# Second mixing: latent products and norms run among the delta rule's state steps, attention heads among the first branch's tiles; equal shapes together

## The reference, cut to what matters

```python
proj = h @ w_in[l]
q_lat, kv_lat, k_pe, gq, gk, gv, ga, gb, gz, gates = jnp.split(proj, split_at, axis=-1)
y_mla = mla_branch(q_lat, kv_lat, k_pe, ...) @ w_o_mla[l]
y_gdn = gated_deltanet_branch(concat([gq, gk, gv]), ga, gb, gz, ...) @ w_o_gdn[l]
mixed = (gate_mla * y_mla + gate_gdn * y_gdn) @ w_out[l]
# mla_branch, 8 heads:
q = (rmsnorm(q_lat, g_q) @ w_uq)        # 768 -> 8 x (128 + 64), the 64 rotated by position
kv = (rmsnorm(kv_lat, g_kv) @ w_ukv)    # 256 -> 8 x (128 keys + 128 values)
s = (qn @ k_nope.T + qp @ k_pe.T) * scale; p = softmax(mask(s)); o = p @ v
# gated_deltanet_branch, 8 chunks of 64 tokens, 8 heads, one step per chunk:
v_new = u_n - w_n @ state
o = qd @ state + a_n @ v_new
state = state * cd + kd.T @ v_new
# then o = rmsnorm(o, g_out) * silu(z)
```

## Time and profile before

| | before |
|---|---|
| median of 3 executions | 3745.99 us (3742.91 to 3747.77) |
| profiled execution, its own time | 3751.27 us |
| span of the profile | 3749.5 us |
| TensorE busy, share of the span | 3443.9 us, 92% |
| VectorE busy | 2047.9 us, 55% |
| ScalarE busy | 1329.6 us, 35% |
| mean granted TensorE clock | 0.924 |
| share of the chain that ended last: TensorE, VectorE, ScalarE, DMA | 79%, 11%, 4%, 3% |

### The profile page before, as it was taken

How to read it: one execution, slowest core, us unless ns; L and a number is a source line. 1 busy time by engine, 2 the same in 40 slices (tenths; PEclk the granted TensorE clock), 3 DMA queues, 4 the chain that set the end, 5 groups by cost and what they waited for, 6 DMA issues and landing times.

```text
span 3749.5 us, 41096 instructions
## 1 busy us (share of the span) xinstructions
PE 3443.9 (92%) x16313; PEld 2794.3 (75%) x16313; DVE 2047.9 (55%) x3550; ACT 1329.6 (35%) x2342; POOL 522.2 (14%) x541
## 2 busy tenths in 40 slices
PE   5897997998999999999899987989988798889998
PEld 3466577998888888888788866877775563578887
DVE  2455598785887887888555335554432323343332
ACT  1222123886444444444322234545340212223221
POOL 0000100995222222221000000000000000000000
PEclk9886899999999999999799988999995697799999
DMA  5330523456998989997255321222211121022222
GB/s 176 136 107 12 174 95 108 176 199 248 349 324 324 330 322 332 319 330 269 95 186 185 126 94 59 71 70 85 71 49 37 55 68 68 31 82 91 100 91 79
DMA packets 189679, 574.02 MB, mean 153 GB/s; under 512 B 16368, under 2 KB 80496, under 8 KB 171056
## 3 DMA queue, kind: packets, MB, share of 16 engines
q1 hardware_dynamic: 152160, 369.80, 28.4%
q0 software_dynamic: 37328, 201.61, 14.6%
HBM read 523.69 MB, written 47.64 MB: 152 GB/s over the span
## 4 chain that ended last, share of the span: by engine, by line
PE 79%; DVE 11%; ACT 4%; DMA 3%; POOL 1%; issue 1%; SPq 0%; DVEq 0%; ACTq 0%; POOLq 0%
PE ps L228 10%; PE ps L229 10%; PE ps L230 10%; PE ps L237 5%; PE ps L1439 5%; PE ps L1440 5%; PE ps L1438 5%; PE ps L1200 3%; PE ps L1202 3%; PE ps L1201 3%; PE ps L312 2%; PE ps L168 1%; DVE Wl L220 1%; DMA hidden_dram<-peerg_HS 1%; PE ps L509 1%; PE ps L2150 1%
## 5 line engine op out<-in xcount | busy, mean ns | idle before, releaser
L220 DVE TENSOR_TENSOR Wl<-W,Wh 128x1024 fp32r<-128x1024 f32 x363 | 438.2, 1208 | 740.1 <-ACT Wh L214 740.1
L214 ACT ACTIVATE Wh<-W 128x1024 fp32r<-128x1024 f32 x363 | 377.6, 1041 | 595.9 <-PE ps L230 575.1
L1200 PE MATMUL ps<-peer_Hh,Wh 128*128 128x384 f32 x1024 | 348.6, 340 | 14.1 <-DVE Wl L220 14.1
L1202 PE MATMUL ps<-peer_Hh,Wl 128*128 128x384 f32 x1024 | 345.0, 337 | 0.0
L1201 PE MATMUL ps<-peer_Hl,Wh 128*128 128x384 f32 x1024 | 344.6, 337 | 0.0
L1438 PE MATMUL ps<-peerv_VH,peer_HTh 128*128 128x512 f32 x768 | 299.8, 390 | 9.6 <-DVE peer_HTl L1501 9.6
L1440 PE MATMUL ps<-peerv_VH,peer_HTl 128*128 128x512 f32 x768 | 301.1, 392 | 0.0
L1439 PE MATMUL ps<-peerv_VL,peer_HTh 128*128 128x512 f32 x768 | 301.1, 392 | 0.0
L1408 POOL DMA_INDIRECT peerv_UV<-peer_uv,peer_EX x128 | 209.4, 1636 | 657.7 <-DVE peer_Y L1475 607.8
L228 PE MATMUL ps<-f_Hh,Wh 128*128 128x512 f32 x672 | 262.2, 390 | 2.2 <-DVE Wl L220 2.2
L230 PE MATMUL ps<-f_Hh,Wl 128*128 128x512 f32 x672 | 261.5, 389 | 0.0
(11 more groups left out here) (467 smaller groups left out, 6709.5 us busy)
## 6 DMA issues: line engine op xcount, KB each, us to landing
W<-peer_u SPq DMA_DIRECT2D x128, 512.0 KB, 7.2
peerv_VR<-peer_v SPq DMA_DIRECT2D x128, 512.0 KB, 5.3
gates_dram<-peerg_GB SPq DMA_DIRECT2D x12, 2048.0 KB, 7.3
peerv_GR<-gates_dram SPq DMA_DIRECT2D x32, 768.0 KB, 8.6
f_AW<-w_ada POOLq DMA_DIRECT2D x48, 512.0 KB, 4.2
W<-w_gate SPq DMA_DIRECT2D x44, 512.0 KB, 3.2
W<-w_up SPq DMA_DIRECT2D x44, 512.0 KB, 3.2
swa_AW<-w_ada POOLq DMA_DIRECT2D x32, 512.0 KB, 4.8
```

The lines of the kernel that those rows point to most:

```text
L214: A.then_inc(e.activation(w_parts(i)[0], w_raw(i), ACT.Copy), ("w_hi", i))
L220: V.then_inc(e.tensor_tensor(lo, w_raw(i), hi.bitcast(F32), SUB), ("w", i))
L1200: e.matmul(o, hi[:, k, :], H2[0][:, k, 0:TD], start=k == 0, stop=False)
L1202: ins = e.matmul(o, lo[:, k, :], H2[0][:, k, 0:TD], start=False, stop=k == 7)
```

## The change

- **delta**: the key latents and the rotary row are no longer sent to DRAM but kept (KL, KP). Behind the rows, `keys_*` computes the key latents' norm and the first four uk tiles, one piece for each round of the last heads' steps.
- **state**: within a step the QD products now come directly behind the WT products, and the AN products directly behind the KD products. `FILL[n]` names two lists for step n: work done ahead of VN's products and work done behind them (uk 4 to 7, the query latents' norm as "lsq" and "bc", the rotary row, uq 0 to 7, and the output norm of the token block that is already complete: "red" sum and root, "on" scaling, "ot" transposes). `BEHIND` is the rest, after the last step. All fills take the banks 6 and 7 in turn. ZG holds two blocks of the gate at a time instead of all eight.
- **heads**: the stages b1 and latent are gone from the lists; `weave` gets a third task that runs one piece after the two heads' pieces. The first branch's tiles are issued in rounds 3, 8, ... 38. A head now has three banks instead of four (one for the transposes instead of two), the branch has two. The scores' rotary product takes all 128 partitions, with keys of which the other head's half is zero (KP and KP2, parted by `keys_apart`).
- SyncE's and GpSimd's lists follow; x comes back from DRAM behind the last transposes instead of behind the latent products.

Core of the diff:

```diff
-def weave(tasks, width):
-    todo, live = list(tasks), []
+def weave(tasks, width, side=()):
+    todo, live, side = list(tasks), [], iter(side)
     while todo or live:
         while todo and len(live) < width:
             live.append(todo.pop(0))
         for g in list(live):
             if next(g, "end") == "end":
                 live.remove(g)
+        next(side, None)
+    run(side)
...
+    t_uk = [weight("w_ukv_k", nb, 256, "plain") for nb in range(8)]
+    t_uq = [weight("w_uq_2", nb, 768, "plain") for nb in range(8)]
+    TAIL = [("uq", 8), ("uv", 0), ("uq", 9), ("uv", 1), ("uv", 2), ("uq", 10), ("uv", 3), ("uq", 11)] \
+        + [("uv", c) for c in range(4, 8)]
+    t_tail = {key: weight("w_uq_2", key[1], 768, "plain") if key[0] == "uq" else weight("w_ukv_v", key[1], 256, "plain")
+              for key in TAIL}
...
+    def keys_pe(e):
+        yield
+        V.wait_ge(e, ("nx", 14))
+        lat_norm_pe(e, "k", 2, 6)
+        yield
+        yield
+        V.wait_ge(e, ("nx", 15))
+        lat_norm_bc(e, "k", 7)
+        yield
+        V.wait_ge(e, ("k", "ln"))
+        for n in range(4):
+            if n < 2:
+                (V if ROWS[NROW - 2 + n][0] == "qkv" else A).wait_ge(e, ("row_out", NROW - 2 + n))
+            else:
+                A.wait_ge(e, ("lat", "uk", n - 2))
+            pe_plain(e, ps((NROW + n) % 2), t_uk[n], 2, 128, KL, ("lat", "uk", n))
+            yield
...
+    FILL = [([("uk", 4)], [("uk", 5)]),
+            ([("uk", 6)], [("lsq", 0), ("uk", 7)]),
+            ([("rope", 0)], [("red", 0), ("bc", 0), ("uq", 0)]),
+            ([("uq", 1), ("on", 0)], [("ot", 0, 0), ("uq", 2)]),
+            ([("uq", 3)], [("ot", 0, 1), ("red", 1), ("uq", 4)]),
+            ([("uq", 5), ("on", 1)], [("ot", 1, 0)]),
+            ([("uq", 6)], [("red", 2), ("ot", 1, 1)]),
+            ([("uq", 7), ("on", 2)], [("ot", 2, 0), ("ot", 2, 1)])]
+    BEHIND = [("red", 3), ("uq", 8), ("uv", 0), ("on", 3), ("uq", 9), ("rope", 1), ("uv", 1), ("ot", 3, 0), ("ot", 3, 1),
+              ("uv", 2), ("uq", 10), ("rope", 2), ("uv", 3), ("uq", 11), ("rope", 3), ("uv", 4), ("uv", 5), ("rope", 4),
+              ("uv", 6), ("uv", 7)]
+    ITEMS = [x for pair in FILL for part_ in pair for x in part_] + BEHIND
+    BANKED = [x for x in ITEMS if x[0] not in ("red", "on")]
...
+    def bank_free(e, x):
+        n = BANKED.index(x)
+        if n < 2:
+            return
+        y = BANKED[n - 2]
+        if y[0] in ("uk", "uq"):
+            A.wait_ge(e, ("lat",) + y)
+        elif y[0] == "uv":
+            V.wait_ge(e, ("lat",) + y)
+        elif y[0] in ("rope", "ot"):
+            V.wait_ge(e, y)
+        else:
+            V.wait_ge(e, ("q", {"lsq": "lr1", "bc": "ln"}[y[0]]))
...
+    def fill_pe(e, items):
+        for x in items:
+            kind, n = x[:2]
+            if kind in ("red", "on"):
+                continue
+            bank_free(e, x)
+            o = bank_of(x)
+            if kind == "uk":
+                pe_plain(e, o, t_uk[n], 2, 128, KL, ("lat", "uk", n))
+            elif kind == "uq":
+                V.wait_ge(e, ("q", "ln"))
+                pe_plain(e, o, t_uq[n] if n < 8 else t_tail[x], 6, 128, QL, ("lat", "uq", n))
+            elif kind == "uv":
+                i = t_tail[x]
+                w_landed(e, i)
+                w = w_raw(i).rearrange("p (k m) -> p k m", k=2)
+                for sl in sl4:
+                    for k in range(2):
+                        ins = e.matmul(o[:, sl], KL[:, k, sl], w[:, k, :], start=k == 0, stop=k == 1)
+                PE.then_inc(ins, ("w", i), ("lat", "uv", n))
+            elif kind == "lsq":
+                lat_norm_pe(e, "q", 6, 6 + BANKED.index(x) % 2)
...
+    def fill_act(e, items):
+        for x in items:
+            kind, n = x[:2]
+            if kind in ("uk", "uq"):
+                PE.wait_ge(e, ("lat",) + x)
+                to = KN[:, n, :] if kind == "uk" else QN[:, n, :] if n < 8 else QP[:, n - 8, :]
+                A.then_inc(e.activation(to, bank_of(x), ACT.Copy), ("lat",) + x)
...
+    def keys_apart(e):
+        V.then_inc(e.memset(KP2[0:64, :], 0.0))
+        V.then_inc(e.tensor_copy(KP2[64:128, :], KP[64:128, :]))
+        V.wait_ge(e, V.n)
+        V.then_inc(e.memset(KP[64:128, :], 0.0), "kp2")
+    def fill_dve(e, items):
+        for x in items:
+            kind, n = x[:2]
+            if kind == "lsq":
+                PE.wait_ge(e, ("k", "lbc"))
+                lat_norm_dve(e, "q", 6, 6 + BANKED.index(x) % 2)
+            elif kind == "bc":
+                lat_scale_dve(e, "q", QL, 6, "g_q_lat_2", 6 + BANKED.index(x) % 2)
+            elif kind == "rope":
+                to, y = rope_x(n), OT[:, 0, :] if n == 0 else RY[:, n % 2, :]
+                PE.wait_ge(e, ("rope", n))
+                V.then_inc(e.tensor_tensor(y, bank_of(x), sin, MUL))
+                V.then_inc(e.tensor_tensor(to, to, cos, MUL))
+                V.wait_ge(e, V.n)
+                V.then_inc(e.tensor_tensor(to, to, y, ADD), ("rope", n))
+            elif kind == "uv":
+                PE.wait_ge(e, ("lat", "uv", n))
+                V.then_inc(e.tensor_copy(VTK[:, :, n * 128:n * 128 + 128], v4(bank_of(x))), ("lat", "uv", n))
+            elif kind == "red":
+                r = r32[:, 8 * n:8 * n + 8]
+                A.wait_ge(e, ("osq", n))
+                V.then_inc(e.tensor_reduce(r, GT2[n % 2], AX.X, ADD), ("ored", n))
+                V.wait_ge(e, ("ored", n))
+                V.then_inc(e.tensor_scalar(r, r, 1.0 / 128, EPS, MUL, ADD), ("or1", n))
+            elif kind == "on":
+                r = r32[:, 8 * n:8 * n + 8]
+                O = Ut[:, :, sl4[n]]
+                A.wait_ge(e, ("or2", n))
+                V.then_inc(e.reciprocal(r, r))
+                V.wait_ge(e, V.n)
...
+    def state_pe(e):
+        behind(e, "delta")
+        pw, pd, po = ps(0, 2), ps(2, 2), ps(4, 2)
         for n in range(8):
             tb, p0, S0, S1 = chunk(n)
             c0, c1 = n * 64, n * 64 + 64
             V.wait_ge(e, ("S", n))
-            pw, pd, po = ps(0, 2), ps(2, 2), ps(4, 2)
             for h in range(8):
                 ins = e.matmul(pw[p0:p0 + 64, h * 128:h * 128 + 128], WTt[:, h, c0:c1], S0[:, h, :], start=True, stop=True)
             PE.then_inc(ins, ("pw", n))
-            yield
+            if n:
+                A.wait_ge(e, ("o", n - 1))
+            for h in range(8):
+                e.matmul(po[p0:p0 + 64, h * 128:h * 128 + 128], QD[:, h, c0:c1], S0[:, h, :], start=h % 4 == 0, stop=False,
+                         skip_group_check=True)
+            fill_pe(e, FILL[n][0])
             V.wait_ge(e, ("vn", n))
             if n < 7:
                 for h in range(8):
                     ins = e.matmul(pd[:, h * 128:h * 128 + 128], KDt[p0:p0 + 64, h, sl4[tb]], VN[p0:p0 + 64, h, :],
                                    start=True, stop=True)
                 PE.then_inc(ins, ("pd", n))
-            if n:
-                A.wait_ge(e, ("o", n - 1))
             for h in range(8):
-                o = po[p0:p0 + 64, h * 128:h * 128 + 128]
-                e.matmul(o, QD[:, h, c0:c1], S0[:, h, :], start=True, stop=False, skip_group_check=True)
-                ins = e.matmul(o, AN[p0:p0 + 64, h, tb * 128 + p0:tb * 128 + p0 + 64], VN[p0:p0 + 64, h, :],
+                ins = e.matmul(po[p0:p0 + 64, h * 128:h * 128 + 128],
+                               AN[p0:p0 + 64, h, tb * 128 + p0:tb * 128 + p0 + 64], VN[p0:p0 + 64, h, :],
                                start=False, stop=True, skip_group_check=True)
             PE.then_inc(ins, ("po", n))
...
         for n in range(8):
             tb, p0, S0, S1 = chunk(n)
                 PE.wait_ge(e, ("po", n - 1))
...
                                        ps(0, 2)[p0:p0 + 64, :].rearrange("p (h m) -> p h m", h=8), SUB), ("vn", n))
-            yield
+            fill_dve(e, FILL[n][0])
             if n < 7:
                 PE.wait_ge(e, ("pd", n))
                 V.wait_ge(e, ("S", n))
...
+    br1 = Branch("b1", t_b1, t_b2[0:2], 8, OP1, GATE1, None, (6, 7))
+    br2 = Branch("b2", t_b2, t_wo2[0:2], 0, H4, GATE2, YP, (4, 5, 6, 7))
...
-            PE.then_inc(e.matmul(S, QP[r0:r0 + 64, h // 2, sl4[q]], KP[r0:r0 + 64, 0:w_], start=False, stop=True),
+            PE.then_inc(e.matmul(S, QP[:, h // 2, sl4[q]], (KP, KP2)[h % 2][:, 0:w_], start=False, stop=True),
...
             V.wait_ge(e, ("pn", h, q))
-            if q >= 2:
-                A.wait_ge(e, ("pt2", h, q - 2))
+            if q:
+                A.wait_ge(e, ("pt2", h, q - 1))
             for kb in range(q + 1):
-                ins = tr(e, ps(b + 2 + q % 2)[:, sl4[kb]], P_[:, q % 2, sl4[kb]])
...
+    def heads_sp(e):
+        for i in t_b1[0:4]:
+            w_load(e, i)
+        PE.wait_ge(e, ("ot", 3, 1))
+        x_back.then_inc(e.dma_start(X_t, XD), "x")
+        for i in t_b1[4:]:
+            w_load(e, i)
+    def branch_pe(e):
+        for r in range(39):
+            if r % 5 == 3:
```

(48 more changed lines are left out.)

500 lines of the change are left out of this document (194 added, 306 removed).

## The result

The changed kernel takes **3637.69 us** (median of 4 runs, 3636.41 to 3644.05) against 3746.88 us for the kernel before, timed with it (4 runs, 3742.91 to 3747.85): a ratio of 0.9714, 95% interval 0.9697 to 0.9731. It is 109.2 us faster; forecast were 93 us and 3653 us. The profiled execution took 3638.46 us with a span of 3636.6 us and a mean granted clock of 0.948 (before: 3751.27, 3749.5 and 0.924).

What follows compares the result with a forecast made beforehand. TensorE is busy but at a low granted clock where 128-row and 64-row products alternate. Stages 149+48+148 = 345 us against 442.6, minus 97.6; plus 8, minus 3: minus 93, giving 3653 us, range 3615 to 3708.

Steps and rivals of the forecast that it cites:

- state steps: busy above 121 us of work: State steps: low clock adds 17 us, from 2 us per step for 64-row products and 1 for the sums.
- state steps: stalls: State steps: 11 us of TensorE waits, 7 of them for the scaled query latents in step 2.
- latent products, to the first mask: Latent products left behind the steps: 40 us of work, 3 of waits, 5 before the first mask; 48 us.
- heads: busy above 107 us of work: Heads with the first branch: 12 us for the clock, since a pair is busy only 0.79 of its time.
- heads: stalls: Heads with the first branch: 29 us of stalls, four pairs taking 136 us with 107 of TensorE work.
- end of the delta stage, with the two weight splits gone: End of the delta stage: key norm and four uk add 8 us; removing two weight splits saves 3.
- shared formula: Whole stretch takes 268(1+s)+w: s is the share of work added by low clock, w all waits.
- the rival in which the clock stays up: Whole stretch: no clock loss, s = 0, 316 us, minus 122 in all, 3624 us; chance 0.19.
- The price of a tile: Heads: each 5.45 us branch tile hides about 1.2 us in a wait, costing 4.3, plus 0.7 for VectorE.
- swing for good: Whole stretch: clock swings between levels around short idles, s = 0.30, 396 us, minus 42, 3704 us; chance 0.17.
- The waits did not double: Whole stretch: rival with all waits doubled to 96 us, stretch 393, minus 45, 3701 us; chance 0.15.
- The slower case: Fills and tiles, cut into 2 to 5 us pieces, lose the high clock; s from 0.46 on; chance 0.04.

Runs made afterwards that it cites:

- run 9: Changed kernel with the fills of steps 1 and 2 reordered: two uk tiles moved between bc and uq 0, latents scaled before squares are summed; 3635.97 us.
- run 4: Changed kernel with the QD and AN products taking turns again behind the KD products, fills kept; 3659.47 us.
- Run 7: Changed kernel with all fills in the same order behind the eight state steps, none within them; 3641.17 us.
- run 6: Changed kernel with the first branch's eight tiles in one piece ahead of the attention heads instead of among them; 3648.3 us.
- run 2: Kernel before, with only the rotary score products widened to 128 rows by 64 zero rows; 3720.56 us.
- run 11: Changed kernel with each branch tile cut into two halves, in rounds 0, 2, 4 and 6 of each 11; 3615.51 us.
- run 3: Kernel before, with both the regrouped state-step products and the 128-row score products, all stages as before; 3653.0 us.
- run 8: Changed kernel with no fill within the state steps and the branch tiles ahead of the heads; 3645.68 us.
- run 1: Kernel before, with only the state-step order changed: QD behind WT, AN behind KD, nothing filling the steps; 3680.36 us.
- run 5: Changed kernel with the rotary score products on 64 rows again, tiles still among the heads; 3647.84 us.
- run 10: Run 9 plus the query norm's sums as six 512-column products with a matrix of ones, so bc goes; 3627.14 us.
- run 12: Changed kernel with the other fill order, the wide sums and the half tiles together; 3596.54 us.

## Why the prediction was right

The mechanism held: TensorE's low level under alternating small products was the cost, and the new order takes it away. Term by term, for the stretch from the first state product on:

| term | forecast | measured |
|---|---|---|
| state steps: busy above 121 us of work | 17 | 128.1 - 121 = 7.1 |
| state steps: stalls | 11 | 136.4 - 128.1 = 8.3 |
| latent products, to the first mask | 48 | 44.6 + 5.5 = 50.1 |
| heads: busy above 107 us of work | 12 | 117.5 - 107 = 10.5 |
| heads: stalls | 29 | 141.2 - 117.5 = 23.7 |
| whole stretch | 345 | 327.7 |
| end of the delta stage, with the two weight splits gone | +8 - 3 = +5 | +9.4 - 3.4 = +6.0 |

In the shared formula, s came out at 290.2/268 - 1 = 0.08 (forecast 0.11), with 290.2 the busy time of the four windows, and w at 327.7 - 290.2 = 37.5 us (forecast 48). The median, 3637.7 us, lies as far from the forecast (3653) as from the rival in which the clock stays up (3624); s, 0.08 between 0.11 and 0, is nearer to the forecast, and the waits came out shorter than either had them.

*The state steps.* Right: KD and AN at 1.98/8 and 1.90/8 = 0.25 and 0.24 us a product, and one wait for the scaled query latents in step 2, 6.4 us for the 7 named. The mis-sized term is the clock's: "KD and AN in a row are 4 us of 64-row products, as the dropping ones were", 2 us a step. Steps 3 to 7 lose nothing (1.00 throughout). What is lost lies where the forecast had 1 us, and in the first step: the sums run 10.4 us instead of 6.7, the uk tile behind them 3.37 instead of 1.7, "uq 0" 7.39 us behind the wait instead of 5.2, and the first WT products 3.53 instead of 1.9. The 6.7 us stood among the work at the high clock, but that row holds 3.7 us at 1.00 and 3 us at 0.50 (run 9); all at the low level the sums are 10.4 us. That 64-row products in a row would lower the clock was a wrong guess at which property counts; run 4 shows that in this surrounding not even the alternation does.

*The norm.* Its hole is gone. Run 7 shows that its cover did not depend on the fills being among the steps: moved behind them, all together, the time is within the interval of the changed kernel.

*The heads.* 141 us for 148; the pairs (L2571 to L2571 in the chain) take 34.4, 32.7 and 33.6 us, where the sum had 34 + a quarter of the clock's 12. The price of a tile, "4.3 us each" after hiding 1.2 us and 0.7 for VectorE, 5.0 in all, comes near the measured (143.6 - 99.8)/8 = 5.5, but partly by luck: run 6 shows that the hiding was not there (without tiles the wait is 20.9 us, with them 19.0), and the charge for VectorE and the 12 us for the clock made up for it. The sum came out because the heads without tiles are as fast as forecast (24, measured 23.5 to 25.0 in run 2, with its clock of 0.92) and the tiles' 44 us are simply added.

*The rivals.* The clock did not stay up altogether (3624 us), nor swing for good (3704): 0.92 in the heads against 0.68 before. When run 11 takes most of the idle time away (24.2 to 7.1 us), the clock goes from 0.92 to 0.99; with it the share lost is 10.5/107 = 0.1 and not 0.43. (0.43 was the share of the whole stretch; the heads alone had lost 110.9 - 63 = 48 us, near the 46 that the prediction set.) The rule of the Trainium skill that stood for that rival ("TensorE: Matmul & The Clock Gate", section "A second HAM failure mode: psum-queue depth-cycling") is half borne out by these numbers: the clock does fall around short idles, but it costs a fraction of what that rival made of them. The waits did not double, they came out below the forecast. The slower case needed the fills and tiles to lose their clock; in pieces of 2 to 5 us they kept it.

*What the sum did not show.* It did not separate the parts' worth. In the interval, the order of the products and the zero rows bring 94.6 us by themselves (run 3), the weaving 8.3 (run 8), the rest of the rearrangement 11.8, less the 6.0 us that the delta stage gives back; together 108.7. And order and weaving stand in for each other: the order is worth 70 us in bare steps (run 1) and 19 in filled ones (run 4), the zero rows 29 us in bare heads (run 2) and 8 in filled ones (run 5). That the order brings the clock back is shown; through what is shown only for the heads (run 2, the row counts). In the steps it may be the turns, the wait on VN that goes with them, or both. What in the filled stages keeps the clock up under alternation, the 512-column shapes of the fills or that TensorE has no idle time there, is not settled: no run here filled the stages with anything else.

## What to carry to other kernels

When TensorE is busy and slow, read the granted clock of a short stretch before looking for waits: putting equal shapes together, padding rows with zeros included, is a few lines and gave nine tenths of this gain. When work is woven in to hide waits, compare the wait itself with and without it (20.9 against 19.0 us here); whole tiles in every fifth round hid almost nothing, half tiles behind the scores of each pair's first rounds took the wait to nothing. Do not explain one fall of the clock from one trace: look for the same place in a run that shares the code (runs 10 and 12). Find the wait that ends last after the change and look at what stands before it in its queue: moving two fills took 4 us off it.

## What the runs showed of the hardware

- Forty-eight one-column products keep TensorE busy throughout, and yet the granted clock falls to 0.50 while they run, also when it stood at 1.00 before them and nothing was waited for (before: 1.00 for 3.5 us of them, then 0.50). Begun at 0.50 they stay there to their end, 10.37 us (the changed kernel); six 512-column products in their place began at 0.50 and saw it rise within 8.43 us (run 10).
- A QD and an AN product in turns cost 0.72 us a pair at the high level, against 0.46 us in two groups (run 4), with the clock at 0.98. Begun low, they stayed at 0.50 for 9.8 us without a wait (before); begun high, at 1.00 for 5.7 us (run 4).
- Score products of 128 and 64 rows in turns ran at 0.68 of the clock over the stage; with the 64 rows filled up to 128 with zeros, at 0.92, with more idle time (run 2).
- VectorE's reciprocal on 128x512 took 3.35 us, where the multiplication and addition on the same shape (the tensor_scalar ahead of it) took 0.69 us (run 10).
- Behind the same wait of 1.21 us, and in the same code, the AN products ran low in one execution, 3.67 us (run 10), and high in another, 1.96 us (run 12).
